# Token scales and the residual carried through memory instead of through TensorE

## The chip, the cores and the metric

One core of a Trainium2 chip runs the whole program. The metric is the device time of one execution in microseconds (us). The engines are named as the profile names them: PE is TensorE, DVE is VectorE, ACT is ScalarE, POOL is GpSimd and SP is SyncE, which here only issues transfers.

## The reference, cut to what matters

```python
h = _rms(x, g_mix)                         # x: 512 tokens x 1024 features
z = h @ w_in                               # za, zu, zv, zq and three gates
ya = gelu(s5(za)); ya = (ya * sigmoid(ya @ w_glu + b_glu)) @ w_a_out
yb = sgu(zu, zv) @ w_b_out
yc = attention(zq, rms(mem, g_mem) @ w_kv) @ w_c_out
merged = gates[0] * ya + gates[1] * yb + gates[2] * yc
x = x + merged @ w_out                     # x1, the residual
hf = _rms(x, g_ffn)
x = x + (silu(hf @ w_gate) * (hf @ w_up)) @ w_down
return _rms(x, g_final)
```

Everything is float32. `_rms` multiplies each token's row by the reciprocal root of its mean square (the token scale) and each feature by a gain.

## The kernel before, in words

**Layout.** Activations lie with features over the 128 partitions and tokens along the row (`xT`, `h_hi`, `h_lo`), so a token scale has to stand in every partition. The root mean squares of x and of mem come from token-major copies (`xtok`, `mtok`), where one token is one partition: `trstd` is 128x4, `mtrstd` 128x2. To get them into every partition as `rstd` (128x512) and `mrstd` (128x256), `token_scale` on DVE multiplies the identity by the scales (`xdiag`, `mdiag`), `wide_rows` on PE multiplies that by a matrix of ones (L1596), and DVE copies the bank out (L1090, L1129). PE does this in the middle of the zv tiles.

**Matmuls.** Each float32 product is made of three matmuls, hi by hi, hi by lo, lo by hi (`product`, L1557 to L1559; `step` in the last phase, L1926 to L1928). A weight tile of 128x1024 arrives by SP in `raw` (two slots), ACT rounds it to `w_hi` (`round_weights`, L561), POOL subtracts to get `w_lo` (L505 in halves, L500 whole), and PE uses it. Tiles are numbered: zv is T_ZV (4) to 7, then q and k from T_QK (8), v and u from T_VU (16), the gates and branch outputs from T_J1 (24), w_out at T_WO, gate and up at T_FF, w_down at T_DN. ACT and DVE each run one list written out by hand, and an instruction that waits holds all behind it. In the first part ACT also copies `uT` into chunks (`chunked`, L621, four calls a group) once DVE has scaled it with `rstd` (`za_taken`).

**Last phase.** w_down is multiplied by a Winograd-like scheme: eleven units (k = 0 to 10, `load_unit`, `round_unit`, L548, L551), eleven three-piece steps, then two passes over four groups of 2, 3, 3 and 3 pieces (`GROUPS`). Each unit's tile is loaded to one of five slots; `UNIT_SLOT` says which, and SP waits until the slot's last user is through. POOL makes the low part of nine units and DVE of units 6 and 8. For the later steps ACT rounds (`round_three`, L888) and DVE makes the low part (`low_three`), and PE waits for it (`ready3`). The residual x1 stays in `xT` to the end, features over partitions. `turn_x1` on PE transposes it with the identity into the accumulators (L1914, 32 transposes of 128x128 in four places), so that the sum of product and x1 stands in the bank; DVE adds the partial sums `s1`, `s5`, `u2`, `u3`, ACT squares, and DVE scales the four token blocks out.

Of the kernel before, what the change touches and what calls it, by code (L numbers as in the profile page):

```python
# [70 lines left out]

TWO_PI = 2 * np.pi
# [8 lines left out]
def build(nc, xt_d, xtok_d, mem_d, mtok_d, small_d, sgu_d, row_d, w_d, mix_d, half_d, out_d):  # L81
# [7 lines left out]
    with ExitStack() as ctx:  # L89
# [39 lines left out]
        y_out = at("y_out", o_x, [P, 4, D])  # L129

        raw_c = at("raw_c", o_s + (4 * C_BRE + 63) // 64 * 64, [P, TILE])
        raw_d = [at(f"raw_d{i}", o_h + 12288 + 4096 * i, [P, TILE]) for i in range(2)]
        unit_raw = [raw[:, 0, :], raw[:, 1, :], raw_c[:, :], raw_d[0][:, :], raw_d[1][:, :]]
        UNIT_SLOT = (0, 1, 2, 3, 4, 0, 1, 2, 0, 1, 2)
# [6 lines left out]
        quarter = (((u3, 0), (s5, 0)), ((u3, 1), (s5, 1)), ((s1, 0), (u2, 0)), ((s1, 1), (u2, 1)))  # L141
# [70 lines left out]
        xdiag = at("xdiag", o_g, [P, 4, P])  # L212
        mdiag = at("mdiag", o_g + 2048, [P, 2, P])
# [28 lines left out]
        def sems(names):  # L242
# [19 lines left out]
        tok_sq, tok_std, diag_x, diag_m, wide_x, wide_m, rstd_ready, mrstd_ready = sems(  # L262
            "tok_sq tok_std diag_x diag_m wide_x wide_m rstd_ready mrstd_ready")
# [21 lines left out]
        unit_loaded = [sem(f"unit_loaded{i}") for i in range(5)]  # L285
# [5 lines left out]
        x1_turned, dn_done, o_sq, o_bias, o_std, o_rec, x2g_ready = sems(  # L291
            "x1_turned dn_done o_sq o_bias o_std o_rec x2g_ready")
# [13 lines left out]
        OUT_BANK = ((0, 2), (1, 3), (4, 6), (5, 7))  # L306
# [44 lines left out]
        def _(sp):  # L351
# [73 lines left out]
            def load_unit(k):  # L425
# [3 lines left out]
                elif 3 <= k < 5:  # L429
                    sp.wait_ge(w_used, T_DN)  # L430
                elif k >= 5:
                    unit_split(sp, {5: 0, 6: 1, 7: 2, 8: 5, 9: 6, 10: 7}[k])
# [34 lines left out]
            for k in range(6, 10):  # L467
                load_unit(k)
            load_three(0)
            load_unit(10)  # L470
# [84 lines left out]
        def _(act):  # L555
# [1568 lines left out]
```

## Time and profile before

| | us |
|---|---|
| median of 3 runs (lowest, highest) | 777.4 (776.43, 777.72) |
| the profiled execution, its own time | 777.84 |
| its span | 776.1 |
| PE busy, share of the span | 765.6, 99% |
| DVE busy | 541.6, 70% |
| ACT busy | 354.3, 46% |
| POOL busy | 315.8, 41% |

The span is what the trace covers; 1.7 us of the profiled time lie outside it. A share is an average over stages with different limits. In a timeline row the first number is the start in us from the span's start, the second the length of the row's instructions together, and a bracket tells how long the engine stood idle before it and what ended that. Matmuls overlap in the pipeline, so the distance from one start to the next is their cost on PE, and not the length of the row.

### The profile page before, as it was taken

How to read it: one execution, taken by the hardware profiler on the slowest of the kernel's cores; microseconds unless marked ns; L12 is line 12 of the kernel's file. 1: busy time of each engine (PE TensorE's matmuls, PEld its weight loads, DVE VectorE, ACT ScalarE, POOL GpSimd, SP SyncE). 2: the span in 40 equal slices, each digit the busy share in tenths (PEclk: the TensorE clock that was granted, in tenths of full speed). 3: DMA queues.
4: the chain of work that ended last, by engine and by line, in shares of the span. 5: the costliest groups of instructions: out<-in, count | busy, mean ns of one | idle time of the engine just before them, and what ended most of it. 6: DMA issues, size and time to landing. Idle time of an engine off the chain costs nothing.

```text
span 776.1 us, 9751 instructions
## 1 busy us (share of the span) xinstructions
PE 765.6 (99%) x3576; PEld 630.8 (81%) x3576; DVE 541.6 (70%) x729; ACT 354.3 (46%) x526; POOL 315.8 (41%) x169
## 2 busy tenths in 40 slices
PE   9999999999999999999999999999999999999996
PEld 7778887788888888888888888888888888778885
DVE  6999997684848484345865677777776777635686
ACT  6896567644545434543433333332323233444463
POOL 4456646233333333444444344534444453920000
PEclk9999999999999999999999999999999999999999
DMA  7744332132222432232324465666756557677852
GB/s 274 297 142 135 110 109 86 31 102 82 82 82 82 132 139 82 82 108 84 106 96 146 147 206 180 214 230 203 228 186 196 204 200 246 196 246 249 280 179 109
DMA packets 39667, 121.98 MB, mean 157 GB/s; under 512 B 4048, under 2 KB 4176, under 8 KB 37840
## 3 DMA queue, kind: packets, MB, share of 16 engines
q1 hardware_dynamic: 39488, 121.26, 47.1%
q8 instruction: 21, 0.34, 0.2%
q10 hardware_dynamic: 144, 0.26, 0.1%
q14 instruction: 14, 0.11, 0.0%
HBM read 104.99 MB, written 16.52 MB: 157 GB/s over the span
## 4 chain that ended last, share of the span: by engine, by line
PE 78%; DVE 13%; ACT 3%; issue 2%; DMA 2%; POOL 1%; SPq 0%; POOLq 0%; DVEq 0%; ACTq 0%
PE bank L1557 21%; PE bank L1558 21%; PE bank L1559 21%; PE bank L1926 4%; PE bank L1928 4%; PE bank L1927 4%; DVE pow_tmp L969 3%; DVE tab_tmp L969 1%; DVE s5p L969 1%; PE bank L1798 1%; DMA xT<-xt_dram 1%; DMA raw<-mix_dram 1%; DVE m_lo L974 1%; ACT prob L655 1%; DVE h_lo L974 0%
## 5 line engine op out<-in xcount | busy, mean ns | idle before, releaser
L500 POOL TENSOR_TENSOR w_lo<-raw,w_hi 128x1024 fp32r<-128x1024 f32 x90 | 219.1, 2434 | 298.1 <-ACT w_hi L561 298.1
L561 ACT ACTIVATE w_hi<-raw 128x1024 fp32r<-128x1024 f32 x112 | 118.6, 1060 | 309.1 <-PE bank L1559 302.3
L1557 PE MATMUL bank<-h_hi,w_hi 128*128 128x512 f32 x608 | 238.2, 392 | 0.5 <-DVE th L969 0.4
L1559 PE MATMUL bank<-h_hi,w_lo 128*128 128x512 f32 x608 | 236.7, 389 | 0.0
L1558 PE MATMUL bank<-h_lo,w_hi 128*128 128x512 f32 x608 | 236.6, 389 | 0.0
L1557 PEld LDWEIGHTS bank<-h_hi,w_hi 128*128 128x128 f32 x608 | 114.1, 188 | 25.5 <-DVE th L969 1.3
L1559 PEld LDWEIGHTS bank<-h_hi,w_lo 128*128 128x128 f32 x608 | 114.1, 188 | 23.9
L1558 PEld LDWEIGHTS bank<-h_lo,w_hi 128*128 128x128 f32 x608 | 114.2, 188 | 23.3 <-issue 0.2
L505 POOL TENSOR_TENSOR w_lo<-raw,w_hi 128x512 fp32r<-128x512 f32 x48 | 67.2, 1422 | 56.3 <-ACT w_hi L561 49.7
L969 DVE TENSOR_TENSOR mix<-mix 128x512 f32<-128x512 f32 x44 | 47.2, 1072 | 10.5 <-DMA mix<-w_dram 9.4
L969 DVE TENSOR_TENSOR lo<-raw,hi 128x1536 fp32r<-128x1536 f32 (+1 forms) x19 | 33.3, 1757 | 28.8 <-ACT hi L888 28.8
L969 DVE TENSOR_TENSOR ops<-parts,ops 128x1024 f32 x11 | 26.2, 2384 | 27.9 <-ACT ops L858 24.2
L888 ACT ACTIVATE hi<-raw 128x1536 fp32r<-128x1536 f32 (+1 forms) x19 | 27.3, 1441 | 35.3 <-PE bank L1928 35.3
L969 DVE TENSOR_TENSOR th<-bank,rstd 128x512 f32<-128x512 f32 x16 | 10.9, 682 | 30.5 <-PE bank L1559 30.5
L755 ACT ACTIVATE yaf<-bank 32x128 f32<-32x128 f32 x64 | 24.9, 389 | 4.5 <-PE bank L1773 3.8
L969 DVE TENSOR_TENSOR parts<-parts,silu 128x512 f32<-128x512 f32 x11 | 24.1, 2195 | 1.4
L1557 PE MATMUL bank<-mg_hi,w_hi 128*128 128x512 f32 x64 | 25.0, 391 | 0.0
L1559 PE MATMUL bank<-mg_hi,w_lo 128*128 128x512 f32 x64 | 24.9, 389 | 0.0
L1558 PE MATMUL bank<-mg_lo,w_hi 128*128 128x512 f32 x64 | 24.9, 389 | 0.0
L969 DVE TENSOR_TENSOR parts<-parts,odd 128x256 f32<-128x256 f32 x11 | 24.3, 2213 | 0.4
L1408 DVE SCALAR_TENSOR_TENSOR h_lo<-xT,small,h_hi 128x512 fp32r<-128x512 f32 x8 | 18.1, 2265 | 9.0 <-ACT h_hi L574 9.0
L969 DVE TENSOR_TENSOR odd<-bank,rstd 128x512 f32<-128x512 f32 x11 | 7.6, 690 | 18.4 <-PE bank L1559 18.4
(297 smaller groups left out, 1391.7 us busy)
## 6 DMA issues: line engine op xcount, KB each, us to landing
raw<-w_dram SPq DMA_DIRECT2D x112, 512.0 KB, 3.4
mix<-w_dram SPq DMA_DIRECT2D x11, 1024.0 KB, 7.7
mix_dram<-mix SPq DMA_DIRECT2D x11, 1024.0 KB, 6.4
raw<-w_dram SPq DMA_DIRECT2D x32, 256.0 KB, 3.9
raw<-mix_dram SPq DMA_DIRECT2D x28, 256.0 KB, 3.9
half_dram<-odd SPq DMA_DIRECT2D x11, 256.0 KB, 7.9
second<-half_dram SPq DMA_DIRECT2D x3, 768.0 KB, 6.0
raw<-mix_dram SPq DMA_DIRECT2D x3, 768.0 KB, 4.3
```

Source lines behind the costliest of these rows:

```text
L500: nc.gpsimd.tensor_tensor(w_lo[:, s, :], raw[:, s, :], fv(w_hi[:, s, :]), ALU.subtract).then_inc(w_ready, 1)
L505: return nc.gpsimd.tensor_tensor(w_lo[:, s, c], raw[:, s, c], fv(w_hi[:, s, c]), ALU.subtract)
L561: nc.scalar.activation(w_hi[:, slot, :], raw[:, slot, :], ACT.Copy).then_inc(w_rounded, 1)
L755: ins = nc.scalar.activation(dst[:, :, i], bank[7][32 * i:32 * i + 32, q * NC:(q + 1) * NC], ACT.Gelu_apprx_tanh)
L888: nc.scalar.activation(hi3[u % 2][:, 0:pieces(u), :], raw3[u % 3][:, 0:pieces(u), :], ACT.Copy).then_inc(rounded3, 1)
L969: return V.tensor_tensor(out, a, b, op)
L1557: mm(out, a[0], b[0], start=first, stop=False)
L1558: mm(out, a[0], b[1], start=False, stop=False)
L1559: return mm(out, a[1], b[0], start=False, stop=last)
L1926: mm(bank[b][:, :], a[0], w[0], start=first, stop=False)
L1927: mm(bank[b][:, :], a[0], w[1], start=False, stop=False)
L1928: return mm(bank[b][:, :], a[1], w[0], start=False, stop=last)
```

## The change

The token scales no longer pass through PE. DVE only takes the reciprocal; ACT issues a transfer of `trstd` to memory (`keep_scale`, 512 single floats), and, after rounding mem, a second transfer that reads the 512 floats back into all 128 partitions (`spread_scale`). The same is done for mem around the chunk copies. ACT waits for the first transfer before it issues the second.

The residual no longer passes through PE either. After x1 is complete DVE transposes it in 32x32 blocks (16 instructions of 128x256), SP stores it to memory (eight transfers), and in the loop's second turn SP loads it token-major into `y_out` (one transfer of 2 MB). For the blocks to come out right the features of x1 are permuted through the rows and columns of the weights (`ORDER`, on the host side of the weights' layout). In the last phase DVE adds x1 from `y_out`.

Beside this the order is changed in places: two weight roundings on ACT stand earlier, the first gate waits for three instead of four `sgu_taken`, DVE's last table step is split around the v copies, the units get seven slots instead of five, and in the second group of each pass PE does all matmuls on rounded weights before those that need the low part (`behind_short`).

```diff
+            def keep_scale(rec, n, t0, t1, kept):
+                act.wait_ge(rec_ready, n)
+                nc.scalar.dma_start(scale_d[t0:t1, :].rearrange("t p -> p t"), rec, allow_slow_non_contiguous=True).then_inc(kept, 16)
+            def spread_scale(dst, kept, t0, t1, wide):
+                act.wait_ge(kept, 16)
+                nc.scalar.dma_start(dst, scale_d[t0:t1, :].rearrange("t p -> (t p)").unsqueeze(0).to_broadcast(
+                    [P, P * (t1 - t0)])).then_inc(wide, 16)
+            keep_scale(trstd[:, :], 1, 0, 4, kept_x)
             act.wait_ge(mem_loaded, 16)
             for k in range(KD):
                 round_tile(norms["m"], m_hi, memf, C_GMEM, k)
+            spread_scale(rstd[:, :], kept_x, 0, 4, wide_x)
             round_weights(T_ZV + 1)
...
+            round_weights(T_ZV + 2)
             act.wait_ge(za_taken, KB)
-            round_weights(T_ZV + 2)
             chunked(0)
             round_weights(T_ZV + 3)
+            keep_scale(mtrstd[:, :], 2, 4, 6, kept_m)
             chunked(1)
+            spread_scale(mrstd[:, :], kept_m, 4, 6, wide_m)
...
             round_weights(T_VU + 5)
+            round_weights(T_VU + 6)
             softmax_scale(2)
             gelu_u(1)
-            round_weights(T_VU + 6)
...
+            def store_x1(h):
+                sp.wait_ge(x1_turned, h + 1)
+                for i in range(4):
+                    sp.dma_start(x1_d[KD * h:KD * (h + 1), :, i, :].rearrange("j a f -> a j f"),
+                                 x1_sq[h][32 * i:32 * i + 32, :, :, :].rearrange("a j k b -> a j (k b)")
+                                 ).then_inc(x1_moved, 16)
...
+                if i == 1 and j < 2:
+                    store_x1(j)
+                if i == 2 and j == 0:
+                    sp.wait_ge(x1_moved, 16 * 8)
+                    sp.dma_start(y_out[:, :, :], x1_d.rearrange("(t j) a i f -> (j a) t (i f)", t=4)
+                                 ).then_inc(x1_moved, 16)
...
+            for h in range(2):
+                for k in range(KD):
+                    ins = V.transpose(x1_sq[h][:, :, k, :], xT[:, k, h * HALF:(h + 1) * HALF].rearrange(
+                        "p (j a) -> p j a", a=32))
+                ins.then_inc(x1_turned, 1)
...
-        UNIT_SLOT = (0, 1, 2, 3, 4, 0, 1, 2, 0, 1, 2)
+        UNIT_SLOT = (0, 1, 2, 3, 4, 5, 6, 0, 1, 2, 6)
...
-            pe.wait_ge(sgu_taken, 4)
+            pe.wait_ge(sgu_taken, 3)
...
-            turn_x1(0, 0)
-            turn_x1(1, 0).then_inc(x1_turned, 1)
+            pe.wait_ge(sums_ready, 1)
             for g, (k0, k1) in enumerate(GROUPS):
                 u = PAIRS + 4 + g
+                if g == 1:
+                    behind_short(u, 0, 0, k0, k1)
+                    continue
```

ACT in the first part, before (the first `w_hi` row is tile T_ZV + 1; `m_hi` is mem rounded, `uc` are the chunk copies):

```order
L574 ACTIVATE m_hi<-memf,small 128x256 x8
L561 ACTIVATE w_hi<-raw 128x1024
L583 ACTIVATE mtok,tssq<-mtok 128x1024 x2
L570 ACTIVATE mtstd<-tssq,eps 128x2
L561 ACTIVATE w_hi<-raw 128x1024
L621 ACTIVATE uc<-uT 32x4x128 x4
L561 ACTIVATE w_hi<-raw 128x1024
L621 ACTIVATE uc<-uT 32x4x128 x4
L561 ACTIVATE w_hi<-raw 128x1024
```

and the same stretch of ACT now:

```order
L632 DMA scale_dram<-trstd 128x4x1
L596 ACTIVATE m_hi<-memf,small 128x256 x8
L636 DMA rstd<-scale_dram 128x512
L583 ACTIVATE w_hi<-raw 128x1024
L605 ACTIVATE mtok,tssq<-mtok 128x1024 x2
L592 ACTIVATE mtstd<-tssq,eps 128x2
L583 ACTIVATE w_hi<-raw 128x1024
L655 ACTIVATE uc<-uT 32x4x128 x4
L583 ACTIVATE w_hi<-raw 128x1024
L632 DMA scale_dram<-mtrstd 128x2x1
L655 ACTIVATE uc<-uT 32x4x128 x4
L636 DMA mrstd<-scale_dram 128x256
```

Four issues of transfers have come into ACT's list; the rounding between `mtstd` and `uc` now stands ahead of the wait for `za_taken`, where it stood behind it.

SP in the last phase, before (`raw_49` are slots 0 and 1, `raw_c_68` is slot 2, `raw3_0` belongs to the three-piece steps):

```order
L435 DMA raw_c_68<-w_dram 128x512
L436 DMA raw_c_68<-mix_dram 128x512
L435 DMA raw_49<-w_dram 128x512
L436 DMA raw_49<-mix_dram 128x512
L435 DMA raw_49<-w_dram 128x512
L436 DMA raw_49<-mix_dram 128x512
L444 DMA raw3_0_77<-mix_dram 128x512
L445 DMA raw3_0_77<-mix_dram 128x512
L446 DMA raw3_0_77<-w_dram 128x512
L435 DMA raw_c_68<-w_dram 128x512
L436 DMA raw_c_68<-mix_dram 128x512
```

and now (`raw_e_74` is the new slot 6):

```order
L458 DMA raw_e_74<-w_dram 128x512
L459 DMA raw_e_74<-mix_dram 128x512
L458 DMA raw_49<-w_dram 128x512
L459 DMA raw_49<-mix_dram 128x512
L458 DMA raw_49<-w_dram 128x512
L459 DMA raw_49<-mix_dram 128x512
L458 DMA raw_c_70<-w_dram 128x512
L459 DMA raw_c_70<-mix_dram 128x512
L458 DMA raw_e_74<-w_dram 128x512
L459 DMA raw_e_74<-mix_dram 128x512
L467 DMA raw3_0_81<-mix_dram 128x512
```

The loads of units 9 and 10 wait for earlier users of their slots than before, and the last unit's load stands ahead of the three-piece loads.

DVE between the two passes, before (`lo` is `low_three`; `s` and `u` are the partial sums):

```order
L969 TENSOR_TENSOR u_73<-bank,s_71 128x512 x2
L969 TENSOR_TENSOR lo_0_82<-raw_0_77,hi_0_80 128x1536
L969 TENSOR_TENSOR u_74<-bank,u_73 128x512 x2
L969 TENSOR_TENSOR u_73<-u_73,s_72 128x1024
L969 TENSOR_TENSOR lo_1_83<-raw_1_78,hi_1_81 128x1536
L969 TENSOR_TENSOR u_73<-bank,u_73 128x512 x2
L969 TENSOR_TENSOR s_72<-s_72,u_74 128x1024
L969 TENSOR_TENSOR lo_0_82<-raw_2_79,hi_0_80 128x1536
L969 TENSOR_TENSOR s_72<-bank,s_72 128x512 x2
```

and now:

```order
L1005 TENSOR_TENSOR u_77<-bank,s_75 128x512 x2
L1005 TENSOR_TENSOR lo_0_86<-raw_0_81,hi_0_84 128x1536
L1005 TENSOR_TENSOR u_78<-bank,u_77 128x512 x2
L1005 TENSOR_TENSOR y_out<-y_out,u_77 128x2x512
L1005 TENSOR_TENSOR lo_1_87<-raw_1_82,hi_1_85 128x1536
L1005 TENSOR_TENSOR y_out<-bank,y_out 128x512 x2
L1005 TENSOR_TENSOR y_out<-y_out,u_78 128x512 x2
L1005 TENSOR_TENSOR lo_0_86<-raw_2_83,hi_0_84 128x1536
L1005 TENSOR_TENSOR y_out<-y_out,u_78 128x2x512
```

The list is the same up to the second `lo`; the sums go to `y_out`, and the additions that read `s_72` have become additions to x1.

## Rows read from the trace of the kernel before

**Rows 1.** The page: busy time, share of the span, number of instructions

```profile
PE 765.6 (99%) x3576; PEld 630.8 (81%) x3576; DVE 541.6 (70%) x729; ACT 354.3 (46%) x526; POOL 315.8 (41%) x169
```

**Rows 2.** Groups of PE by shape: busy us, mean ns, idle before

```profile
L1914 PE MATMUL bank<-small,xT 128*128 128x128 f32 x32 | 4.2, 273 | 0.0
...
L1596 PE MATMUL bank<-xdiag,ones 128*128 128x512 f32 x2 | 1.1, 644 | 0.0
...
L1596 PE MATMUL bank<-mdiag,ones 128*128 128x256 f32 x2 | 0.7, 417 | 0.4 <-issue 0.4
```

**Rows 3.** Timeline of ACT, first part: start, length, row, idle before

```profile
27.79 3.31 ACT L574 ACTIVATE m_hi<-memf,small 128x256 fp32r<-128x256 f32 x8
...
36.92 1.06 ACT L561 ACTIVATE w_hi<-raw 128x1024 fp32r<-128x1024 f32 x1 [0.69 <-DVE uT L969]
37.89 4.56 ACT L621 ACTIVATE uc<-uT 32x512 f32<-32x512 f32 x4
...
59.08 1.06 ACT L561 ACTIVATE w_hi<-raw 128x1024 fp32r<-128x1024 f32 x1 [0.43 <-PE bank L1559]
```

**Rows 4.** Timelines of DVE, POOL and PE in the same stretch

```profile
34.40 2.48 DVE L969 TENSOR_TENSOR uT<-bank,rstd 128x512 f32<-128x512 f32 x4
36.81 5.32 DVE L974 SCALAR_TENSOR_TENSOR m_lo<-memf,small,m_hi 128x256 fp32r<-128x256 f32 x8
```

```profile
60.22 5.88 POOL L505 TENSOR_TENSOR w_lo<-raw,w_hi 128x512 fp32r<-128x512 f32 x4 [1.92 <-ACT w_hi L561]
```

```profile
61.94 0.47 PE L1557 MATMUL bank<-h_hi,w_hi 128*128 128x512 f32 x1
```

**Rows 5.** Transfers by line: count, size, median us from issue to landing

```profile
mtok<-mtok_dram SPq DMA_DIRECT2D x1, 1024.0 KB, 10.8
```

```profile
out_dram<-y_out ACTq DMA_DIRECT2D x1, 256.0 KB, 2.8
```

```profile
772.92 0.38 ACTq L959 DMA_DIRECT2D out_dram<-y_out  x1
```

**Rows 6.** Timelines of ACT and PE around tile T_VU + 6

```profile
118.28 1.99 ACT L561 ACTIVATE w_hi<-raw 128x1024 fp32r<-128x1024 f32 x2
```

```profile
118.85 1.89 PE L1673 MATMUL bank<-kT,qT 128*128 128x256 f32 x8
121.17 0.50 PE L1557 MATMUL bank<-w_hi,m_hi 128*128 128x512 f32 x1 [0.43 <-POOL w_lo L505]
```

**Rows 7.** PE at the first gate, T_J1

```profile
142.59 0.50 PE L1557 MATMUL bank<-h_hi,w_hi 128*128 128x512 f32 x1 [0.43 <-DVE th L969]
```

**Rows 8.** DVE's reciprocal ahead of the gate and up loop

```profile
432.20 3.35 DVE L1416 RECIPROCAL rstd<-std 128x512 f32<-128x512 f32 x1 [9.28 <-ACT std L570]
```

**Rows 9.** Timelines of PE and ACT in the units

```profile
683.45 0.39 PE L1927 MATMUL bank<-lo_c,ops 128*128 128x512 f32 x1
683.68 0.39 PE L1928 MATMUL bank<-hi_c,ops 128*128 128x512 f32 x1
684.18 0.50 PE L1926 MATMUL bank<-w_hi,ops 128*128 128x512 f32 x1
...
686.84 0.39 PE L1928 MATMUL bank<-w_hi,ops 128*128 128x512 f32 x1
688.13 0.50 PE L1926 MATMUL bank<-w_hi,ops 128*128 128x512 f32 x1 [0.90 <-POOL w_lo L551]
```

```profile
681.69 1.06 ACT L879 ACTIVATE w_hi<-raw 128x1024 fp32r<-128x1024 f32 x1 [2.09 <-DMA raw<-mix_dram]
```

**Rows 10.** PE at the first of the four places of turned x1

```profile
693.90 1.06 PE L1914 MATMUL bank<-small,xT 128*128 128x128 f32 x8
694.72 0.48 PE L1926 MATMUL bank<-hi,op 128*128 128x512 f32 x1
```

**Rows 11.** DVE's low parts for steps 13 and 17

```profile
742.98 1.75 DVE L969 TENSOR_TENSOR lo<-raw,hi 128x1536 fp32r<-128x1536 f32 x1
```

```profile
759.55 1.75 DVE L969 TENSOR_TENSOR lo<-raw,hi 128x1536 fp32r<-128x1536 f32 x1
```

More of the change, by code:

```diff
@@ L466, in _ @@
             store_half(PAIRS - 1)
-            for k in range(6, 10):
+            for k in range(6, PAIRS):
                 load_unit(k)
             load_three(0)
-            load_unit(10)
             load_three(1)
@@ L1477, in _ @@
                 V.tensor_copy(s5[:, j, :], bank[6 + j][:, :]).then_inc(s5_ready, 1)
[L1478 to L1479 removed]
+            low_three(2)
+            dve.wait_ge(x1_moved, 16 * 9)
+            dve.wait_ge(s5_ready, 2)
+            go(tt(x1_two(2, 1), x1_two(2, 1), s5[:, :, :], ALU.add))
+            low_three(3)
+            go(tt(x1_two(0, 1), x1_two(0, 1), s5[:, :, :], ALU.add))
+            low_three(4)
+            dve.wait_ge(s1_ready, 2)
+            go(tt(x1_two(2, 0), x1_two(2, 0), s1[:, :, :], ALU.add))
             for g in range(4):
@@ L1625, in _ @@
                 za_step(k)
-            def zv_step(j, cs):
-                for c in cs:
-                    product(bank[4 + c][:, :], [x[:, c * P:(c + 1) * P] for x in h(j)], weight(0, j, 0, WB, WB),
-                            j == 0, False)
-            pe.wait_ge(w_half, T_ZV + 1)
-            zv_step(0, range(3))
-            pe.wait_ge(diag_x, 1)
-            wide_rows(7, xdiag[:, :, :], T, wide_x)
-            tile_ready(T_ZV)
-            zv_step(1, range(3))
-            pe.wait_ge(rstd_ready, 1)
-            zv_step(0, (3,))
-            c = 3
-            product(bank[7][:, :], [x[:, c * P:(c + 1) * P] for x in h(1)], weight(0, 1, 0, WB, WB),
-                    False, False).then_inc(w_used, 1)
-            for t in range(1, 4):
+            for t in range(4):
                 pe.wait_ge(w_half, T_ZV + t + 1)
-                if t == 3:
-                    pe.wait_ge(diag_m, 1)
-                    pe.wait_ge(za_taken, KB)
-                    wide_rows(3, mdiag[:, :, :], M, wide_m)
                 for j in range(2):
@@ L1909, in _ @@
             feed(0, 1, ff_u)
-            def turn_x1(t, n, alone=False):
-                for j in range(4):
-                    ins = mm(bank[OUT_BANK[t][n]][:, j * P:(j + 1) * P], xT[:, 4 * n + j, t * P:(t + 1) * P], ident,
-                             start=j == 0, stop=alone and j == 3, is_transpose=True)
-                return ins
             pe.wait_ge(norms["f"]["std"], 1)
@@ L1975, in _, with behind_short @@
                     pe.wait_ge(s5_ready, 2)
-                    turn_x1(2, 1)
-                    turn_x1(3, 1)
                 for j in range(2):
-                    ins = step(6 + j, fourth(k, j), three(k, 2), False, k == PAIRS - 1)
+                    ins = step(6 + j, fourth(k, j), three(k, 2), k == 0, k == PAIRS - 1)
                 ins.then_inc(used3, 1)
             pe.wait_ge(s1_ready, 2)
-            turn_x1(2, 0)
-            turn_x1(3, 0)
+            def behind_short(u, b, c0, k0, k1):
+                pe.wait_ge(rounded3, u + 1)
+                for k in range(k0, k1):
+                    for j in range(2):
+                        a, w = second_half(k, j, c0), three(u, k - k0)
+                        mm(bank[b + j][:, :], a[0], w[0], start=False, stop=False)
+                        mm(bank[b + j][:, :], a[1], w[0], start=False, stop=False)
+                pe.wait_ge(ready3, u + 1)
+                for k in range(k0, k1):
+                    for j in range(2):
+                        a, w = second_half(k, j, c0), three(u, k - k0)
+                        ins = mm(bank[b + j][:, :], a[0], w[1], start=False, stop=False)
+                ins.then_inc(used3, 1)
             for g, (k0, k1) in enumerate(GROUPS):
                 u = PAIRS + g
+                if g == 1:
+                    pe.wait_ge(half_lo, g + 1)
+                    behind_short(u, 4, HALF, k0, k1)
+                    continue
                 pe.wait_ge(ready3, u + 1)
```

130 lines of the change are left out of this document (58 added, 72 removed).

## The prediction

> **What bounds the kernel now.** I read the page first: PE is busy for 765.6 us of a span of 776.1 [rows 1]. No other engine comes near, so time can be gained in two ways only: PE gets fewer matmuls, or the short stretches in which it stands between matmuls become shorter. The groups of PE by shape give what the removed instructions hold [rows 2]. Then I went along PE's timeline and looked where the distance from one start to the next is more than the usual 0.23 us (683.45 to 683.68 in [rows 9]); most of what is left of the 10 us lies at the two ends and is not touched. In the middle there are few such places: tile T_VU + 6 [rows 6], the first gate [rows 7] and units 9 and 10 [rows 9]. At each I asked who was late, and then whether the cover for PE's new, earlier arrival is long enough. That last question decides this case: where PE comes earlier, the engine that feeds it is next.
>
> **The token scales, first part.** Removed from PE: two row pairs with 1.1 and 0.7 us busy and 0.4 us idle, 2.2 us together [rows 2]. Whether they come off the time is told by ACT. From 37.89, the start of the chunk copies, to 58.65, ACT has no idle time at all: the rounding at 59.08 has 0.43 us idle before it [rows 3]. POOL starts on the low part of that tile (T_QK + 2) at 60.22, two tiles of two halves in 5.88 us, so its first half is out at 60.22 + 1.47 = 61.69, and PE starts the tile at 61.94 [rows 4]. So PE already waits here for ACT's list, by a few tenths, and 2.2 us taken away before it only lengthen this wait. What counts is when ACT's list now ends. It starts its copies when DVE has scaled `uT`, at 34.40 + 2.48 = 36.88 now, and after that did one rounding of 1.0 us (36.92), which has been moved ahead of the wait and saves that us. It gets two issues of transfers, which the trace shows at 0.38 us each [rows 5]; with the gap around an issue 0.85 us together. The new start of the copies is the way through memory: ACT can issue the first transfer at 27.8, behind T_ZV's rounding, and is through at 28.2. How long 512 single floats take no row shows. The nearest row is the store that ACT itself issues at the end, 2.8 us on quiet engines; the other bound is the 10.8 us of the mtok load, which was in flight in these same microseconds with the 16 DMA engines nearly full [rows 5]. The new transfer is on ACT's own queue and not behind that load, so I take a value near the lower bound, 4.3 us, landing at 32.5. The rounding of mem ends at 27.79 + 3.31 = 31.1, later than the best case, so the second transfer is issued between 31.1 and 39.0. Mine: 32.5 + 0.4 + 2.4 for the landing = 35.3; DVE needs 2.5 us; copies from 37.85, against 37.89 before. The start of the copies is the same, since the rounding that is gone from 36.92 to 37.89 makes room for the later scale, and the end is later by the two issues: 58.65 + 0.85 = 59.5 against 59.08. **Cost 0.4 us**, bounds -0.2 (copies from 37.3, because the moved rounding itself only ends then) and +6.2 (10.8 us for the first landing, 6.5 later than mine). DVE loses the two diagonals and two copies, and gets the wait; its list had no slack to give PE here.
>
> A rule speaks against this way. The row that bears on it is that no group of transfers in the page has pieces this small. The Trainium skill, DMA: Bandwidth & Descriptors, Rules for kernel authors, says that a strided last dimension becomes one descriptor per element and should be rearranged, and its section Bandwidth gives about 10.5 ns a packet; as an estimate by that page 32 of them on each of 16 engines cost 0.3 us on top of a fixed 2 us, landing at 30.5, and the term would be the lower bound of -0.2. No row here shows which holds.
>
> **Order edits on the way to T_J1.** ACT rounds T_VU + 6 at 118.28, behind a softmax step that waits for DVE; PE has its score matmuls through at 118.85 + 1.89 = 120.74 and then stands 0.43 us [rows 6]. In a run without a stand the next matmul starts some 0.25 us before the last one's end (693.90 + 1.06 against 694.72 in [rows 10]), so the loss is 0.7 us and a start-up of a tenth: 0.8. The rounding now stands ahead of the softmax step and its tile is free since about 112, so all of it goes; next late would be the following tile, rounded at the same time as before and needed 2.7 us later. The first gate waits 0.43 us for the fourth `sgu_taken` [rows 7], worth 0.7 by the same reckoning; it now needs the third, one addition earlier. **Gain 1.5 us**, bounds 0.8 and 1.6. Splitting DVE's table step puts the v copies earlier and nobody waits for the tables: nothing.
>
> **The way of x1.** PE loses 32 transposes, 4.2 us busy [rows 2], in four places of 694.72 - 693.90 = 0.82 us each plus a tenth of start-up [rows 10]; 3.6 us in all. DVE gets 16 transposes. No row shows one; the nearest are eight 128x256 low parts in 5.32 us, 0.67 each, with POOL at work beside them [rows 4], and 256 of the 512 columns that take 0.65 in a PSUM addition, 0.38. That is 6 to 11 us, ahead of the reciprocal, where DVE now stands for 9.28 us [rows 8]. Cover for the rest, at most 1.4 us: PE has 48 matmuls of 0.23, 11 us, from the square sum to the bank that DVE must free, and DVE needs ACT's root, 3.35 for the reciprocal and one multiplication for it, so some 4 us are spare. Nothing. The eight stores stand in SP's list behind a weight load; DVE is through by then. The 2 MB load of the second turn stands ahead of a weight load; the DMA engines have the room (the page's slices show them 0.6 busy in the loop), and a weight tile is loaded well over 5 us before ACT wants it. Nothing, bounds 0 and 2. In the last phase DVE gets three additions to x1 between low parts where it has idle gaps of over 2 us: nothing there.
>
> What the transposes covered is the other half. After the first pass PE has a group of two pieces and one of three, 30 matmuls, 6.8 us, and before also 0.8 us of transposes before step 13. Its low part is ready at 742.98 + 1.75 = 744.73 [rows 11]. All of DVE's list up to there hangs on the last unit of the first pass, not on the transposes, so it does not come earlier. Without the two sets of transposes PE arrives at about 743.7 instead of 745.6: of 1.8 us it keeps 0.8. The same at step 17: low part at 759.55 + 1.75 = 761.3 [rows 11], which moves by the 0.8 only, while PE arrives another 0.8 earlier; it keeps some 0.3 of that. `behind_short` covers only the three-piece steps behind the short group, not these. With the first place whole (0.9): **gain 2.0 us** of 3.6, bounds 1.7 and 3.5.
>
> **The units.** PE starts 0.50 us and 1.29 us after the last matmul at units 9 and 10, so it loses 0.27 and 1.06, with start-up 1.5 us; ACT had waited 2.09 us for unit 9's load [rows 9]. With seven slots both loads are issued by 666 and about 675, and nothing else holds them. **Gain 1.5 us**, bounds 0.3 (POOL's own pace) and 1.6.
>
> **Sum.** 777.84 (own time of the profiled execution) + 0.4 - 1.5 - 2.0 - 1.5 = 773.2. The median of the runs is 0.44 below that execution, so between 772.8 and 773.2; I give 773.0.
>
> **Rivals.** (1) More comes off: ACT's list turns out shorter and the low parts are in time. Then all of 2.2 + 1.5 + 3.6 + 1.5 = 8.8 goes: 769.0. For it: PE is at 99%. Against it: the starts at 61.94 and at step 13. (2) The first scale transfer is slow, 8 us instead of 4.3: ACT stands, and every us is a us of PE: 773.2 + 3.7 = 776.9. For it: full DMA engines and single floats. (3) Slower: it needs over 9 us. ACT stands in its list from 31.1 with the rounding of T_ZV + 1 behind it, DVE stands with all tables behind it, PE at T_QK + 2. At 10.8 us: 773.2 + 6.5 = 779.7; from 8.9 us on (773.2 + 4.6) it is no faster than before. (4) The units' stall is POOL's pace and stays, and the 2 MB load holds one weight tile by a us: 773.2 + 1.2 + 1.0 = 775.4. (5) The change doesn't do what it says: if the transfers were waited for by PE, its waits would name them; the waits stand on DVE and ACT, so I give this nothing.
>
> **How the numbers follow.** Forecast (771.5 to 774.5) 0.55; rival 1 0.14; rival 2 0.12; rival 3 0.08; rival 4 0.11. A measurement of this kernel can tell about 0.2%, 1.6 us, from no change: 775.8 to 779.0 is the same. Rivals 2 and a part of 4 fall in it, and rival 3 above. Faster 0.78, same 0.15, slower 0.07. The range takes in rival 1's end and rival 2's near end: 769.0 to 776.8.
>
> **What would show it.** In the changed profile: the rows on `xdiag`, `mdiag` and `xT` are gone from PE; `uc` copies start at about 37.9 and tile T_QK + 2 at 62.3 on PE; no POOL wait at T_VU + 6; PE waits on DVE's low part at step 13 by about a us; no wait at units 9 and 10; x1's transposes lie in the gap before the reciprocal. I am wrong if ACT's second scale transfer is issued after 34, or if T_QK + 2 starts a us earlier than before.

## The result, and the profile after

The changed kernel takes 782.66 us (median of 6 runs, 781.46 to 785.14) against 777.48 us for the kernel before beside it. The ratio is 1.0074, 95% interval 1.0053 to 1.0094: slower, where 773.0 was forecast. One of the six runs of the kernel before took 1101.2 us; without it their median is 777.40. The profiled execution took 781.46 us, its span is 779.7. It is the fastest of its six, so the two traces lie 3.6 us apart and the medians 5.2.

The page of the changed kernel (as [rows 1]; second line: the clock granted to PE in 40 slices of the span, 9 is full):

```profile
PE 761.7 (98%) x3540; PEld 629.1 (81%) x3540; DVE 540.6 (69%) x744; ACT 354.5 (45%) x526; POOL 314.3 (40%) x169
PEclk9989999999999999999999999999999999999999
```

PE is 3.9 us less busy, and the span is 3.6 us longer: PE stands more. The first step is to find in which stage. I compared where the same instruction starts on PE in both traces:

| PE starts | before | after | lead or lag |
|---|---|---|---|
| tile T_QK + 2 | 61.94 | 71.11 | +9.2 |
| first scores | 87.13 | 96.36 | +9.2 |
| first gate, T_J1 | 142.59 | 149.78 | +7.2 |
| its second matmul | 142.93 | 150.42 | +7.5 |
| first matmul behind the square sum of x1 | 429.31 | 436.80 | +7.5 |
| end of the third step of the units | 672.18 | 679.65 | +7.5 |
| last matmul | 769.62 | 773.27 | +3.6 |

So 9.2 us are lost before T_QK + 2, and 1.7 us (up to the gate's second matmul) and 3.8 us come back later, near the forecast. What makes the change slower lies in the first 71 us. ACT's timeline there (columns as in [rows 3]):

```profile
28.37 0.40 ACTq L632 DMA_DIRECT2D scale_dram<-trstd  x1
28.83 3.31 ACT L596 ACTIVATE m_hi<-memf,small 128x256 fp32r<-128x256 f32 x8 [2.19 <-DVE trstd L1112]
37.65 0.34 ACTq L636 DMA_DIRECT2D rstd<-scale_dram  x1
38.10 1.06 ACT L583 ACTIVATE w_hi<-raw 128x1024 fp32r<-128x1024 f32 x1 [5.96 <-DMA scale_dram<-trstd]
...
44.56 4.59 ACT L655 ACTIVATE uc<-uT 32x512 f32<-32x512 f32 x4 [2.05 <-DVE uT L1005]
...
49.30 0.38 ACTq L632 DMA_DIRECT2D scale_dram<-mtrstd  x1
50.36 4.54 ACT L655 ACTIVATE uc<-uT 32x512 f32<-32x512 f32 x4
57.78 0.33 ACTq L636 DMA_DIRECT2D mrstd<-scale_dram  x1
58.20 1.06 ACT L583 ACTIVATE w_hi<-raw 128x1024 fp32r<-128x1024 f32 x1 [3.30 <-DMA scale_dram<-mtrstd]
...
68.53 1.07 ACT L583 ACTIVATE w_hi<-raw 128x1024 fp32r<-128x1024 f32 x1
```

The 512 floats are issued at 28.37 and ACT is released at 37.65, 9.3 us later; it had stood 5.96 us with the rounding of T_ZV + 1 behind it. The chunk copies (`uc`) start at 44.56, where they started at 37.89 [rows 3]: 6.7 us later. Mem's 256 floats, issued at 49.30, cost the list a second stand of 3.30 us. T_QK + 2 is rounded at 68.53 instead of 59.08. PE in the same stretch, and then its clock (columns: stretch, its length, busy time and number of PE, PEld, DVE, ACT and POOL, granted clock, DMA share, GB/s):

```profile
33.70 0.39 PE L1589 MATMUL bank<-w_hi,h_lo 128*128 128x512 f32 x1
40.55 0.80 PE L1587 MATMUL bank<-w_hi,h_hi 128*128 128x512 f32 x1 [6.46 <-POOL w_lo L527]
41.14 0.63 PE L1588 MATMUL bank<-w_lo,h_hi 128*128 128x512 f32 x1
41.57 0.63 PE L1589 MATMUL bank<-w_hi,h_lo 128*128 128x512 f32 x1
```

```profile
33.00:37.00 4.00, 1.09 (x5) 0.56 (x3) 0.00 (x0) 0.00 (x0) 0.00 (x0) 0.93 0.23 28
37.00:42.00 5.00, 1.45 (x4) 1.17 (x5) 0.00 (x0) 3.87 (x7) 2.50 (x2) 0.50 0.13 52
42.00:46.00 4.00, 4.00 (x11) 3.17 (x10) 3.96 (x7) 1.93 (x3) 2.52 (x2) 0.50 0.80 301
```

PE stands 6.5 us for the low part of T_ZV + 1. That tile's load, issued at 21.61, landed at 36.56, so ACT could not have rounded it before 36.6 even without its wait. While PE stands, the granted clock falls from 1.0 to 0.5 (from 2.4 to 1.2 GHz), and the next matmuls are 0.43 us apart instead of 0.23, up to about 46.6.

One more view belongs to it, the transfers with the time from issue to landing. The first fence has those issued between 26 and 34, the second the weight load issued between 50 and 54, in the changed kernel; the third has the weight load issued between 26 and 34 in the kernel before:

```profile
raw<-w_dram SPq DMA_DIRECT2D x1, 512.0 KB, 8.5
scale_dram<-trstd ACTq DMA_DIRECT2D x1, 2.0 KB, 9.3
```

```profile
raw<-w_dram SPq DMA_DIRECT2D x1, 512.0 KB, 8.2
```

```profile
raw<-w_dram SPq DMA_DIRECT2D x1, 512.0 KB, 4.2
```

The weight loads that are under way beside a store of floats take 4 to 5 us longer: 8.5 instead of 4.2, 8.2 instead of 3.4, and the one issued at 21.6 takes 15.0 instead of 10.8. The DMA engines move little meanwhile: 28 GB/s from 33 to 37, with the store and two weight loads under way. This decides the case, as the experiments show.

The later stages (rows of the changed kernel: DVE's transposes of x1 and its reciprocal; then PE's waits on DVE in the last phase):

```profile
430.34 5.33 DVE L1439 STREAM_TRANSPOSE x_sq<-xT 128x256 f32<-128x256 f32 x16
439.70 3.35 DVE L1445 RECIPROCAL rstd<-std 128x512 f32<-128x512 f32 x1 [4.03 <-ACT std L592]
```

```profile
PE bank L1925 <- DVE lo L1005: 1.2, 2, 0.8
```

### The profile page after: what moved, and what is told of

Its sections match the earlier page's. It is cut to its first block, busy times and chain, and to the rows that moved or that the text cites. A ratio compares the mean times of both kernels' runs of the same rounds, so it can differ in the third digit from the quotient of the medians.

```text
span 779.7 us, 9706 instructions
## 1 busy us (share of the span) xinstructions
PE 761.7 (98%) x3540; PEld 629.1 (81%) x3540; DVE 540.6 (69%) x744; ACT 354.5 (45%) x526; POOL 314.3 (40%) x169
## 4 chain that ended last, share of the span: by engine, by line
PE 87%; DVE 3%; DMA 3%; ACT 3%; POOL 2%; issue 1%; SPq 0%; ACTq 0%; DVEq 0%
PE bank L1587 24%; PE bank L1589 24%; PE bank L1588 24%; PE bank L1925 3%; PE bank L1927 3%; PE bank L1926 3%; DMA scale_dram<-trstd 1%; DMA scale_dram<-mtrstd 1%; POOL w_lo L573 1%; PE bank L1802 1%; PE bank L1677 1%; DVE lo L1005 1%; PE bank L1694 1%; DVE s5p L1005 1%; DMA xT<-xt_dram 1%; POOL lo_c L573 1%
## 5 line engine op out<-in xcount | busy, mean ns | idle before, releaser
L1005 DVE TENSOR_TENSOR mix<-mix 128x512 f32<-128x512 f32 x44 | 44.9, 1020 | 13.3 <-DMA mix<-w_dram 12.2
L1005 DVE TENSOR_TENSOR lo<-raw,hi 128x1536 fp32r<-128x1536 f32 (+1 forms) x19 | 32.5, 1713 | 24.0 <-ACT hi L925 24.0
L1005 DVE TENSOR_TENSOR parts<-parts,silu 128x512 f32<-128x512 f32 x11 | 26.0, 2366 | 1.4
L1005 DVE TENSOR_TENSOR parts<-parts,odd 128x256 f32<-128x256 f32 x11 | 22.3, 2024 | 0.4
L1587 PE MATMUL bank<-w_hi,h_hi 128*128 128x512 f32 x32 | 13.8, 433 | 6.5 <-POOL w_lo L527 6.5
```

Source lines behind the costliest of these rows:

```text
L1005: return V.tensor_tensor(out, a, b, op)
L1587: mm(out, a[0], b[0], start=first, stop=False)
```

## The experiments

Theory A: the whole loss is the way of the scales through memory, and the rest of the change gives what was forecast. Its rival: the other parts cost as well. Its first form, a wait that blocks lists, fell with the experiment on the lists; theory D took its place: the store of single floats is slow and slows all transfers beside it.

### All but the scales

The edit undoes `keep_scale` and `spread_scale` and brings back `token_scale`, `wide_rows` and the two copies:

```diff
-            dve.wait_ge(tok_std, 1)
-            V.reciprocal(trstd[:, :], tstd[:, :]).then_inc(rec_ready, 1)
+            def x_scale():
+                token_scale(4, 1, tstd[:, :], trstd[:, :], xdiag[:, :, :], diag_x)
```

> The changed kernel with both token scales made the old way again (diagonal on DVE, row pair on PE, copy out of the bank), everything else of the change kept. Theory A (the whole loss sits in the way of the scales through memory, the other parts give what I forecast): before 777.5 less 1.5 for the order edits, 2.0 for the way of x1 and 1.5 for the units, so 772.5 us, ratio to before 0.9936, and tile T_QK + 2 on PE at 61 to 62 again. Rival B (the other parts cost as well, for instance the 2 MB load or the transposes): 775 or more. Rival C (the other parts give more, hidden by the loss): under 771.

Measured: 772.4 us, ratio 0.9935 (0.9918 to 0.9952). A second comparison of the same kernel:

> The kernel with the old scales and all else changed, again: 772.4 as in its first comparison.

Measured: 772.22 us, ratio 0.9925 (0.9911 to 0.9938). Theory A holds to a few tenths. Without the scales the change gives 4.8 and 5.7 us, and by the medians the scales take 10.

### The scales alone

The kernel before with only `keep_scale` and `spread_scale` and their waits; the rounding of T_ZV + 2 stands ahead of the wait for `za_taken`, and the row pairs are gone from PE, as in the change.

> The kernel before with only the two token scales sent through memory. Theory A: tile T_QK + 2 on PE starts 9 us later than before (of which up to 0.9 is where PE begins) and nothing later in the program takes it back, so 777.5 + 8.5 to 9.5 = 786 to 787 us, ratio about 1.0115. Rival B (later stages have slack that takes back a part of a late start): 782 to 784. The transfer of the 512 floats lands about 9 us after its issue again, that of the 256 about 8.5.

Measured: 791.67 us, ratio 1.0184 (1.0167 to 1.0201), more than expected. Mem's store landed after 11.3 us, ACT stood 5.33 us for it and not 3.30, and so PE stood a second time long enough for the clock to fall:

```profile
58.00:62.00 4.00, 0.41 (x2) 0.00 (x0) 3.93 (x6) 2.55 (x3) 1.47 (x2) 0.87 0.36 126
62.00:66.00 4.00, 3.81 (x9) 3.07 (x10) 2.85 (x5) 3.93 (x4) 1.46 (x2) 0.50 0.40 114
```

The sign was right. Rival B (slack later on) is out: T_QK + 2 and the first scores start 11.5 us later than before, and the last matmul 11.7. The size was not right: by the medians the same edit costs 10 us in one surrounding and 14 in the other. Of these 4 us the traces show about 2, as much as ACT's second stand is longer. The profiled execution, 789.70 us, is the fastest of the four; what the others lost beyond it is in no trace and stays open.

### Order edits and slots alone

> The kernel before with the order edits and the seven slots of the units only: scales and residual as before. Theory A: the stands at T_VU + 6, at the first gate and at units 9 and 10 go, 1.5 + 1.5: 774.5 us, ratio 0.9961. Rival B: the transposes of x1 that remain meet the low parts of DVE in the same way as before, but one of the stands moves to a later place: 775.5 or more. The difference to the kernel with the old scales is the way of x1 alone, forecast at 2.0.

Measured: 773.86 us, ratio 0.9957 (0.9942 to 0.9971), 3.3 us. In the trace 2.0 us lie between the first scores and the first gate (53.5 us apart, before 55.5), of which 0.3 go again at the gate's second matmul, and 1.9 behind the third step of the units (95.6 us to the last matmul, before 97.4). The kernel with the old scales needs 93.6 us for that last stretch: 2.0 us for the way of x1, as in the sum (1.5 us between the two medians).

### Lists that don't stand

This run was to show that the loss is a blocked list. On ACT the second transfer went behind two roundings, on DVE the low part of mem ahead of the wait:

```diff
-            spread_scale(rstd[:, :], kept_x, 0, 4, wide_x)
             round_weights(T_ZV + 1)
...
             round_weights(T_ZV + 2)
+            keep_scale(mtrstd[:, :], 2, 4, 6, kept_m)
+            spread_scale(rstd[:, :], kept_x, 0, 4, wide_x)
+            round_weights(T_ZV + 3)
             act.wait_ge(za_taken, KB)
```

> The changed kernel with both scales still through memory, but with the lists of ACT and DVE in an order that doesn't stand: on ACT the second transfer of x is issued after the roundings of T_ZV + 1 and T_ZV + 2, the third zv tile and the first q tile are rounded before any chunk copy, half of the chunk copies go later, and mem's first transfer is issued before x's second; on DVE the low part of mem, its reciprocal and the first constants stand ahead of the wait for the spread scale. Theory A (the loss is a wait that blocks lists, not work): PE no longer stands in the zv tiles, and it has 2.2 us of matmuls less than with the old scales; T_QK + 2 at 59 to 61, 770.5 to 772.5 us, below the kernel with the old scales. Rival B (DVE's list or the chunk copies are late afterwards, since both were full in this stretch): 775 to 779. The first transfer lands 9 us after its issue either way.

Measured: 784.48 us, ratio 1.0094 (1.0077 to 1.0111). No gain at all, and theory A in this form falls. ACT had nothing to wait for but its weights, and still rounded T_ZV + 1 at 37.69, only 0.4 us earlier than in the changed kernel:

```profile
37.69 1.06 ACT L583 ACTIVATE w_hi<-raw 128x1024 fp32r<-128x1024 f32 x1 [4.87 <-DMA raw<-w_dram]
...
50.10 1.06 ACT L583 ACTIVATE w_hi<-raw 128x1024 fp32r<-128x1024 f32 x1 [8.00 <-DMA raw<-w_dram]
```

The transfers issued between 40 and 46, while mem's floats were on their way:

```profile
raw<-w_dram SPq DMA_DIRECT2D x2, 512.0 KB, 9.4
sgu<-sgu_dram SPq DMA_DIRECT2D x1, 1024.0 KB, 11.5
rstd<-scale_dram ACTq DMA_DIRECT2D x1, 256.0 KB, 11.7
scale_dram<-mtrstd ACTq DMA_DIRECT2D x1, 1.0 KB, 9.8
```

With mem's store moved next to x's second transfer, that one took 11.7 us instead of 4.3. So waiting elsewhere doesn't help; the store holds up what is under way beside it, on SP's queue and on ACT's own.

### The same way through memory, in pieces of 128 bytes

DVE transposes the 128x4 scales as one 32x32-block transpose of 128x32 (0.21 us), and ACT stores four times four rows of 32 floats:

```diff
-                nc.scalar.dma_start(scale_d[t0:t1, :].rearrange("t p -> p t"), rec, allow_slow_non_contiguous=True).then_inc(kept, 16)
+                for b in range(4):
+                    nc.scalar.dma_start(scale_d[t0:t1, 32 * b:32 * b + 32], rec[32 * b:32 * b + t1 - t0, :]).then_inc(kept, 16)
...
-            V.reciprocal(trstd[:, :], tstd[:, :]).then_inc(rec_ready, 1)
+            link(V.reciprocal(trstd[:, :], tstd[:, :]))
+            V.transpose(t_out[0][:, :], t_in[0][:, :]).then_inc(rec_ready, 1)
```

> The changed kernel, but DVE first transposes the scales in 32x32 blocks, so that they go to memory as 16 pieces of 128 bytes (four transfers of four rows, for mem four of two) and not as 512 (256) single floats; the transfers that spread them are as they were. New theory D (the store of single floats is slow itself and makes every transfer that is under way with it slow: a weight load issued beside it took 15.0, 8.5 and 8.2 us where the kernel before has 10.8, 4.2 and 3.4): the last of the stores lands within 3.5 us of its issue, the weight loads are back at about 10.8 and 4, PE stands under 1 us in the zv tiles, and what is left is the issues on ACT and the spreading: 774 to 777 us. Rival E (a round through memory takes 8 to 9 us in this stretch whatever its pieces are, because the engines are full): landing of 8 us or more, and 781 or more.

Measured: 773.16 us, ratio 0.9939 (0.9916 to 0.9961), 9.5 us less than the changed kernel, with the same bytes, the same spreading and four times the issues. ACT's timeline:

```profile
27.99 1.51 ACTq L636 DMA_DIRECT2D scale_dram<-t_out  x4
29.55 3.31 ACT L599 ACTIVATE m_hi<-memf,small 128x256 fp32r<-128x256 f32 x8 [2.05 <-issue]
32.85 0.36 ACTq L640 DMA_DIRECT2D rstd<-scale_dram  x1
...
38.95 4.57 ACT L659 ACTIVATE uc<-uT 32x512 f32<-32x512 f32 x4 [1.22 <-DVE uT L1009]
```

The second transfer is issued at 32.85, as soon as mem is rounded: the last of the stores, issued at 29.19, needed 3.7 us at most. The weight loads are back at 10.6 and 4.1 us. PE still stands 1.1 us in the zv tiles, a little more than expected. Rival E (the full engines) is out, since they were as full here (323 GB/s from 26 to 34, in the changed kernel 302). The measured time lies a little below the expected range.

### Mem's store alone as single floats

> The kernel with 128-byte stores, but mem's 256 scales go to memory as single floats again, as in the changed kernel. This parts the loss between the two stores. Theory D (both stores count, the second by ACT's wait ahead of the first q tile, 3.30 us in the changed kernel, which my sum did not have at all): x's part is gone, mem's store lands 8 to 9 us after its issue at 43.5, ACT waits some 3 us for it, no stand of PE in the zv tiles above 1.5 us, T_QK + 2 about 3 us later than with both stores in 128 bytes: 773.2 + 2.5 to 3.5 = 775.7 to 776.7. Rival (only the first one matters): 773 to 774.

Measured: 777.53 us, ratio 0.9992 (0.9983 to 1.0002). That is 4.4 us above the kernel before it and 5.1 below the changed kernel: each store has about half of the loss. It is 0.8 us above the expected range. PE stood 2.1 us in the zv tiles, where at most 1.5 were expected, and 3.6 at the first q tile, since ACT stood 4.39 us for mem's store, where some 3 were expected:

```profile
53.68 0.34 ACTq L643 DMA_DIRECT2D mrstd<-scale_dram  x1
54.13 1.06 ACT L586 ACTIVATE w_hi<-raw 128x1024 fp32r<-128x1024 f32 x1 [4.39 <-DMA scale_dram<-mtrstd]
```

### What makes the store slow: probes

Stores of constants on ACT's queue, 17 to 22 us apart, in the rounds of the gates, where the DMA engines are mostly idle. Their victim, the next weight load, is the gauge. It is issued 0.8 to 3.7 us after the store, so where it is issued late, an undisturbed load only tells that the store was over by then.

```diff
+                probe(2 * m)
                 round_weights(t + 4)
...
+                probe(2 * m + 1)
                 round_weights(t + 7)
```

> The kernel with the old scales and all else changed, with eight stores of constants to memory added on ACT's queue in the rounds of the gates, each alone on its queue, two a round: 512 single floats to neighbouring addresses; 256; 128; 128 rows of 16 bytes; 16 rows of 128 bytes; 512 single floats, each 64 bytes from the next; 512 again to neighbouring addresses; one row of 512 bytes. Nobody waits for them. Theory D (cost by piece): about 9 us for 512, 5 to 6 for 256, 3 to 4 for 128 pieces of either size, 2.5 for the last kinds. Rival F (neighbouring single floats collide in memory): 512 spaced floats land clearly sooner than 512 neighbouring ones. Rival E (only the full engines of the first stretch): all under 4 us.

> As the kernel with probes, with other stores, again two a round in this order: 128 single floats, neighbouring; 128 floats 8 bytes apart; 16 bytes apart; 32 bytes apart; 128 pieces of 8 bytes, neighbouring; 128 pieces of 32 bytes, neighbouring; 16 neighbouring floats; 128 floats 64 bytes apart. Read by the weight load issued next, 3.1 to 3.5 us where nothing disturbs it (4.5 for the one near 195), and by how long packets of ACT's queue are seen. Theory F (writes of a few bytes by different engines into the same small block of memory hold each other up): slow (over 8 us) for the neighbouring single floats and the 8-byte pieces, quick from some distance between 16 and 64 bytes on, and slow for the 16 floats too, since the delay was the same for 128 and for 512. Rival D (cost by number of single floats): the 16 floats are quick, all 128 alike.

Two stores of the second probe run, that of 128 neighbouring floats, issued at 152.5, and that of 128 floats 16 bytes apart, issued at 193.4 (landing is the last number):

```profile
probe_dram<-ones ACTq DMA_DIRECT2D x1, 0.5 KB, 7.3
```

```profile
probe_dram<-ones ACTq DMA_DIRECT2D x1, 0.5 KB, 1.4
```

All of them, with the next weight load and, in brackets, the same load in the kernel without probes:

| store | landing, us | load issued after, us | next weight load, us |
|---|---|---|---|
| 512 neighbouring floats | not in the trace | 2.9 and 0.9 | 10.3 (3.2) and 11.0 (4.2) |
| 256 neighbouring floats | not in the trace | 3.6 | 9.4 (3.4) |
| 128 neighbouring floats | 7.3 (second of the two) | 0.9 and 2.9 | 12.1 (4.5) and 8.0 (3.2) |
| 16 neighbouring floats | 2.8 | 0.9 | 5.0 (4.2) |
| 128 floats, 8 bytes apart | 3.3 | 3.5 | 3.8 (3.4) |
| 128 floats, 16 bytes apart | 1.4 | 0.8 | 4.5 (4.5) |
| 128 floats, 32 bytes apart | 1.7 | 3.6 | 3.4 (3.5) |
| 128 floats, 64 bytes apart | 3.1 | 3.6 | 3.3 (3.4) |
| 512 floats, 64 bytes apart | not in the trace | 3.6 | 3.5 (3.5) |
| 128 pieces of 8 bytes, neighbouring | 3.7 | 0.8 | 5.6 (3.3) |
| 128 rows of 16 bytes, neighbouring | not in the trace | 3.7 | 3.5 (3.5) |
| 128 pieces of 32 bytes, neighbouring | 1.7 | 3.6 | 3.5 (3.5) |
| 16 rows of 128 bytes | not in the trace | 0.9 | 3.4 (3.3) |
| one row of 512 bytes | not in the trace | 3.7 | 3.4 (3.4) |

The cost is not the number of pieces: a load issued 3.6 us after the store of 512 floats 64 bytes apart is undisturbed, one issued 3.6 us after 256 neighbouring ones takes 9.4 us, and 128 neighbouring ones disturb as much as 512. It is not the full engines either, which are quiet here. It is how close the small pieces lie: the landing of 128 single floats goes from 7.3 us for neighbours to 3.3 at 8 bytes apart and 1.4 at 16. Theory D as a cost by piece falls, rival F holds in its main line. Two rows don't fit it smoothly: the floats 64 bytes apart need 3.1 us, more than those at 16 and 32, and the 16 neighbouring floats are over in 2.8 us, where rival F said slow. Each row but two rests on one store, and where the load came 3.5 us or more after it, a short disturbance would not show. What the memory does with such writes, no run shows; that stays open.

### Does the fallen clock cost its 3 us?

The changed kernel, with the stand of PE filled by matmuls on zeros:

```diff
+                if t == 1:
+                    for i in range(FILL):
+                        mm(bank[4][:, 0:P], nought[:, :], ones[:, :], start=False, stop=False)
                 pe.wait_ge(w_half, T_ZV + t + 1)
```

> The changed kernel, with 24 matmuls of 128x128 on zeros put on PE ahead of the second zv tile, where it stands for 6.6 us; they add nothing to the sum in the bank. Theory H (of the 9.2 us that the first part loses, about 3 are the clock, which is at half for the matmuls from 40.55 to about 46.6): the granted clock stays at full, the next tile runs at 0.23 us a matmul, 782.7 - 3 = 779.5 to 780.2 us. Rival I (the half clock costs nothing, since the weights come late anyway): 782 to 783.

Measured: 781.75 us, ratio 1.0051 (1.0034 to 1.0068), which overlaps with the changed kernel's own interval. In the stretch that was filled for, the clock stayed at full, but it fell later, behind a second stand (first fence: the stretches from 42 to 44 and from 61 to 64; second: PE's timeline):

```profile
42.00:44.00 2.00, 2.00 (x10) 1.65 (x9) 1.69 (x3) 1.18 (x2) 1.16 (x2) 1.00 0.30 70
...
61.00:64.00 3.00, 3.00 (x9) 2.31 (x8) 2.93 (x4) 2.93 (x4) 1.01 (x1) 0.52 0.36 97
```

```profile
34.64 5.52 PE L1661 MATMUL bank<-ones,nought 128*128 128x128 f32 x48
41.22 0.50 PE L1592 MATMUL bank<-w_hi,h_hi 128*128 128x512 f32 x1 [1.06 <-POOL w_lo L532]
...
60.46 0.47 PE L1592 MATMUL bank<-h_hi,w_hi 128*128 128x512 f32 x1 [2.58 <-POOL w_lo L532]
```

PE then came 2.2 us earlier to the end of the zv tiles (57.49 instead of 59.67) and stood there 2.6 us instead of 0.9 for the first q tile, which hangs on the landing of mem's floats; behind that stand the clock is at 0.5 up to about 64.5, where it stayed at 1.0 in the changed kernel. So the run moved the half clock rather than took it away. T_QK + 2 is rounded by ACT at 68.16, in the changed kernel at 68.53, and the first scores start at 96.31 and 96.36: ACT's list was as late. Theory H falls for the first stretch, whose half clock cost nothing that can be told apart here. What a run without any half clock would take is not shown.

### A version that beats both

Stores of 128 bytes, issued by SP between its weight loads; on DVE mem's low part ahead of the wait; on ACT roundings ahead of chunk copies:

```diff
             round_weights(T_ZV + 2)
+            round_weights(T_ZV + 3)
             act.wait_ge(za_taken, KB)
             chunked(0)
-            round_weights(T_ZV + 3)
+            round_weights(T_QK)
             chunked(1)
-            round_weights(T_QK)
-            chunked(2)
             round_weights(T_QK + 1)
```

> The kernel with 128-byte stores again, with the scale transfers issued by SP instead of ACT, mem's low part on DVE ahead of the wait for the spread scale, and on ACT the third zv tile and the first q tile rounded ahead of chunk copies, with half of the copies later. Theory D (with the single floats gone, what is left of the way through memory are lists, and these can be put right): no stand in the zv tiles and none before T_QK + 2, so PE keeps the 2.2 us of the row pairs that the kernel with the old scales pays: 770.0 to 771.2 us. Rival G (one of the feeding lists is full here whatever its order, DVE's above all): 772 to 774, no better than the kernel with the old scales.

> The kernel with 128-byte stores and lists in order, beside the kernel with the old scales in the same comparison. Theory D: it lacks 2.2 us of matmuls on PE and its stage of the scores begins 2 us after PE's first matmul sooner, so 1 to 2 us less than the old scales, 770.5 to 771.9. Rival G: no difference, the later stages take it back.

Measured: 771.93 us, ratio 0.9925 (0.9909 to 0.9942), and 771.41 us, ratio 0.9912 (0.9896 to 0.9927), beside 772.22 for the old scales in the same comparison. It beats the kernel before and the changed kernel. Against the old scales it is 0.8 us lower by the medians, and the intervals overlap: not told apart. PE has the two row pairs less to do and keeps a part of that at most. The first fence has a line of its waits in this version and, below it, the same line in the first run of the old scales; the second fence has this version's ACT, the third its PE:

```profile
PE bank L1600 <- POOL w_lo L547: 1.4, 2, 0.8
...
PE bank L1588 <- POOL w_lo L529: 0.8, 1, 0.8
```

```profile
33.25 1.06 ACT L603 ACTIVATE w_hi<-raw 128x1024 fp32r<-128x1024 f32 x1 [1.69 <-DMA raw<-w_dram]
```

```profile
35.96 0.50 PE L1600 MATMUL bank<-w_hi,h_hi 128*128 128x512 f32 x1 [0.60 <-POOL w_lo L547]
```

ACT rounds T_ZV + 1 when its load lands, at 33.2, and in the first run of the old scales that load lands at 33.2 too. PE's first zv matmul also starts alike in these two traces, at 29.63 and 29.62, behind a stand of 0.8 to 0.9 us in both, so they can be laid side by side. Where the row pairs were, 1.5 us are gained; 0.7 of it goes in the new stand at 35.96; T_QK + 2 starts 1.0 us earlier and the last matmul 0.7. Taken off PE, the row pairs uncover this load: in these traces the next limit of the stage is the loading. In the second run of the old scales the same load landed at 31.7, and its span is the same as this version's, 769.6 us: how early the first loads land differs by more between runs than what is left to gain.

## Why the prediction was wrong, step by step

**What bounds the kernel.** Right: PE is 98% busy and the time is won or lost in its stands. The question that I called decisive, who feeds PE when it comes earlier, was the right one, but I put it to ACT's and DVE's lists and not to the weight loads that feed them.

**The scales, the step that failed.** The sum has +0.4 for the first part; the traces have +9.2. None of that comes from the start: the first zv matmul is at 28.49, before at 29.18. The step that failed is the landing of the first store, taken at 4.3 us with no row for it, and with it that the store was given no effect on the loads beside it. By its own steps: the first landing was taken at 4.3 us and is 9.3, counted from 28.4 and not 28.2, so 37.65 and not 32.5. The spreading was taken at 2.4 us behind an issue of 0.4, 2.8 in all, and is 4.3 from its issue: 1.5 more. Together the copies start at 44.56, not 37.85: 6.7 us. The third piece, ACT's wait of 3.30 us for mem's store, is missing from the sum; the sentence that ACT's list gains 0.85 us of issues took that landing to be covered by one group of copies. 6.7 + 3.3 is 10.0, of which 0.4 were idle before [rows 3]; T_QK + 2 is rounded 9.5 us later. The 0.85 us for the issues don't show beside it: mem's first one runs while ACT rounds, from 49.30, and its second lies in the stand. Nor was the store's harm to the loads anywhere in the sum: T_ZV + 1 landed 3.8 us later than before, and the run with the lists reordered shows that this alone holds up the zv tiles. My sign that I would be wrong, the second transfer issued after 34, is met.

**The bounds.** 10.8 us for the landing was a wide enough bound for the first transfer alone, and still +6.2 was too low for the term, since the bound was put on one of three things that move together. Rival 3 named what would stand, ACT's list with T_ZV + 1 behind it, but not the slowed loads, and it mis-sized the loss: it has 8.9 us as the point from which nothing is won, and with 9.3 us measured gives 773.2 + 5.0 = 778.2; adding the spreading (1.5) and mem's wait (3.3 - 0.4) gives 782.6 against 781.46 for the profiled execution. Its chance of 0.08 was too low, as the only rows near were of large transfers and none of them held many small pieces.

**The reason given for 4.3 us.** "On ACT's own queue and not behind that load" was wrong in both directions: the queue is separate, the engines are shared, and the harm went from the store to the loads. The Trainium skill, DMA: Bandwidth & Descriptors, Rules for kernel authors, says that queues of different issuers run on the same 16 DMA engines and interleave. That loads on SP's queue went from 4.2 to 8.5 us beside a store on ACT's agrees with it; that a store of 2 KB could do this, while 28 GB/s were moved, that row does not say. The estimate by the packet price in the same page of the Trainium skill, Bandwidth, landing at 30.5, came out 7 us too early: the rule against single-element pieces pointed the right way, and the price does not hold for neighbouring ones. For 128 of them it gives, as an estimate worked out the same way, 2.1 us; measured are 7.3 for neighbours, 3.3 at 8 bytes apart, 1.4 at 16, 1.7 at 32 and 3.1 at 64. The division by 16 engines was my own step; with all 512 packets in a row the same price would give, as an estimate, 7.4 us, but 3.3 for 128 at any distance.

**Order edits.** Forecast 1.5, bounds 0.8 to 1.6; measured 1.7 in three traces (the changed kernel, the old scales, the order edits alone). T_VU + 6 gave 0.8 as said, the gate 0.7 as said (1.0 at its first matmul, 0.3 of it gone at the second), and 0.2 more lie between them.

**The way of x1.** Forecast 2.0; 2.0 in the traces, 1.5 between the medians. The transposes took 5.33 us, 0.33 each and just under my range, inside the 9.28 us [rows 8], of which 4.03 are left. PE waits for DVE's low part at steps 13 and 17, 1.2 us in all, as said.

**The units.** Forecast 1.5, bounds 0.3 to 1.6; 1.9 in the trace. Both stands are gone. Rival 4 is out.

Replacing the one term, 773.2 - 0.4 + 9.2 = 782.0, for a profiled execution of 781.46. With all terms as measured, 777.84 + 9.2 - 1.7 - 2.0 - 1.9 = 781.4.

## What to carry to other kernels

A chain of issue, landing, second issue and second landing holds several unknowns that add up; bound them together, and count every later use of the same chain (mem's) as its own term. Ask of a new transfer also what it does to the loads that run beside it: if a few bytes per partition have to go to memory, transpose them on the chip first, so that they leave in rows (0.21 us on DVE, 9.5 us won here). Where PE stands and its clock falls, look first who is late next; filling the stand won nothing here.

## What the runs showed of the hardware

- A store to memory of 128 or more neighbouring single floats from as many partitions holds up the transfers beside it: 512 KB loads took 7.5 to 12.1 us instead of 3.2 to 4.5. From 33 to 37 the changed kernel moved 28 GB/s with two such loads under way. The same 128 floats 16 bytes apart landed in 1.4 us and left the load issued 0.8 us later at 4.5 us, as without them; 128 neighbouring pieces of 8 bytes are in between (3.7 us, and 5.6 instead of 3.3 for the load).
- The landing of such a store hardly depends on its size from 128 floats on: 9.2 to 10.0 us for 512 floats, 8.4 to 11.3 for 256, 7.3 for 128. For 16 it was 2.8.
- After stands of 6.5, 5.7, 3.8, 3.6 and 2.6 us PE's granted clock was at 0.5 for the next matmuls (2.4 to 1.2 GHz); after stands of 2.1 and 1.1 us it was at 1.0, and so it was with the stand of 6.5 us filled by small matmuls.
- A transpose of 128x256 floats in 32x32 blocks took DVE 0.33 us, one of 128x32 0.21 us.
